# Four modulation blocks moved from the first feed-forward into the second mixer, and eight moved back in the third

## The reference

```python
def modulation(c, w, b):
    m = jnp.einsum("bd,de->be", jax.nn.silu(c), w) + b
    shift, scale, gate = jnp.split(m, 3, axis=-1)
...
for layer in range(DEPTH):                                   # first block: stages 0, 1 and 2, 3
    shift, scale, gate = modulation(c, ada_w[layer, 0], ada_b[layer, 0])
    h = x * (1.0 + scale) + shift
    y = hybrid_mixer(h, ...)                                 # in, SSD + MLA + gating, out
    x = layer_norm(DN_ALPHA * x + (1.0 + gate) * y, ...)
    shift, scale, gate = modulation(c, ada_w[layer, 1], ada_b[layer, 1])
    h = x * (1.0 + scale) + shift
    y = swiglu(h, ...) if layer % 2 == 0 else moe_swiglu(h, ...)
    x = layer_norm(DN_ALPHA * x + (1.0 + gate) * y, ...)
```

## Time and profile before

| | |
|---|---|
| median of 3 runs | 2105.08 us (2104.85 to 2108.06) |
| profiled execution, its own time | 2110.58 us |
| its span | 2108.7 us |
| mean granted clock of TensorE | 0.96 of full |
| busy share | TensorE 94%, VectorE 79%, ScalarE 56% |
| first feed-forward, first product to the next stage's input | 188.95 to 404.76 us |
| second mixer | 404.76 to 531.77 us |
| third mixer up to its last blocks of `wout2` | 1388.85 to 1530.55 us |

### The profile page before, as it was taken

The page is one execution under the profiler, slowest core; times in us unless marked ns, Lnnn a source line. Parts: engine busy times, 40 slices in busy tenths (PEclk is TensorE's granted clock), DMA queues, the critical chain, the costliest instruction groups (busy, mean ns, idle before and its releaser), DMA issues.

```text
span 2108.7 us, 28332 instructions
## 1 busy us (share of the span) xinstructions
PE 1979.9 (94%) x11530; PEld 1713.3 (81%) x11530; DVE 1673.0 (79%) x1753; ACT 1170.4 (56%) x1316; POOL 72.4 (3%) x121
## 2 busy tenths in 40 slices
PE   6989999999799999999999999878899999989999
PEld 6778899886678887887878888668689989869998
DVE  6777889887788998989898888878778886756444
ACT  3544334464567777777777777556444344654432
POOL 6001000000000000000000000000010000000000
PEclk9988999899899999999999999989789998989999
DMA  9754999644499999999999999824359994324552
GB/s 350 267 183 162 349 352 361 215 150 162 166 343 335 352 373 343 341 358 370 324 356 365 361 336 349 310 81 159 120 209 355 353 366 134 121 80 140 180 182 98
DMA packets 251210, 554.37 MB, mean 263 GB/s; under 512 B 10077, under 2 KB 75857, under 8 KB 251073
## 3 DMA queue, kind: packets, MB, share of 16 engines
q1 hardware_dynamic: 247252, 544.13, 72.3%
q0 software_dynamic: 3552, 8.29, 1.2%
q10 hardware_dynamic: 268, 0.07, 0.0%
HBM read 551.40 MB, written 1.05 MB: 262 GB/s over the span
## 4 chain that ended last, share of the span: by engine, by line
PE 75%; DVE 13%; ACT 6%; issue 3%; DMA 3%; SPq 0%; ACTq 0%; DVEq 0%
PE bank L499 22%; PE bank L501 21%; PE bank L500 21%; DVE ring_lo L1960 4%; ACT ring_hi L1263 3%; DVE acc L1900 2%; PE bank L888 1%; PE bank L581 1%; PE bank L550 1%; DMA ring<-in_ffn_w_dram 1%; PE bank L1088 1%; DVE work L2145 1%; DMA ring<-in_w_in_dram 1%; DMA ring<-in_ada_w_dram 1%; PE bank L527 1%
## 5 line engine op out<-in xcount | busy, mean ns | idle before, releaser
L1960 DVE TENSOR_TENSOR ring_lo<-ring,ring_hi 128x2048 fp32r<-128x2048 f32 x417 | 949.5, 2286 | 252.2 <-ACT ring_hi L1263 249.6
L1263 ACT ACTIVATE ring_hi<-ring 128x2048 fp32r<-128x2048 f32 x417 | 794.9, 1913 | 474.3 <-PE bank L501 232.1
L499 PE MATMUL bank<-hh,ring_hi 128*128 128x256 f32 x1152 | 330.3, 287 | 10.4 <-DVE ring_lo L1960 5.6
L500 PE MATMUL bank<-hl,ring_hi 128*128 128x256 f32 x1152 | 328.2, 285 | 0.0
L501 PE MATMUL bank<-hh,ring_lo 128*128 128x256 f32 x1152 | 328.2, 285 | 0.0
L501 PE MATMUL bank<-ring_hi,hl 128*128 128x256 f32 (+2 forms) x768 | 239.1, 311 | 0.0
L499 PEld LDWEIGHTS bank<-hh,ring_hi 128*128 128x128 f32 x1152 | 223.4, 194 | 13.6 <-DVE hl L2024 5.9
L499 PE MATMUL bank<-ring_hi,hh 128*128 128x256 f32 (+2 forms) x672 | 214.2, 319 | 15.6 <-DVE hl L2024 9.2
L499 PE MATMUL bank<-ring_hi,hgh 128*128 128x512 f32 (+1 forms) x576 | 220.4, 383 | 9.0 <-DVE ring_lo L1960 4.0
L500 PEld LDWEIGHTS bank<-hl,ring_hi 128*128 128x128 f32 x1152 | 223.5, 194 | 1.0 <-issue 0.5
L501 PEld LDWEIGHTS bank<-hh,ring_lo 128*128 128x128 f32 x1152 | 223.2, 194 | 0.0
(11 more groups left out here) (425 smaller groups left out, 2788.9 us busy)
## 6 DMA issues: line engine op xcount, KB each, us to landing
ring<-in_moe_w_dram SPq DMA_DIRECT2D x264, 1024.0 KB, 5.2
ring<-in_ada_w_dram SPq DMA_DIRECT2D x48, 1024.0 KB, 7.2
ring<-in_w_mod_dram SPq DMA_DIRECT2D x48, 1024.0 KB, 7.2
ring<-in_w_in_dram SPq DMA_DIRECT2D x40, 1024.0 KB, 6.1
ring<-in_ffn_w_dram SPq DMA_DIRECT2D x33, 1024.0 KB, 5.6
ring<-in_w_gate_dram SPq DMA_DIRECT2D x22, 1024.0 KB, 5.0
ring<-in_w_up_dram SPq DMA_DIRECT2D x22, 1024.0 KB, 5.1
ring<-in_w_down_dram SPq DMA_DIRECT2D x22, 1024.0 KB, 5.0
```

The source lines that it names most:

```text
L499: pe.matmul(ps, xh, wh, start=first, stop=False)
L500: pe.matmul(ps, xh, wl, start=False, stop=False)
L1263: act.activation(ring_hi[i % NH][:, 0:z], ring[n % NS][:, 0:z], ACT.Copy).then_inc(*s.hi(("hi", home(s, i), i)))
L1960: dve.tensor_tensor(ring_lo[n % NS][:, 0:z], ring[n % NS][:, 0:z], hi, ALU.subtract).then_inc(*s.lo(("lo", home(s, i), i)))
```

## The change

Three edits of order, none of arithmetic:

1. The four blocks of stage 3's shift (`mod 3 0 p`) leave the weave of the first feed-forward, which keeps 28 of 32. In the second mixer a new function `put_behind` places them with the four blocks of stage 3's gate (`mod 3 2 p`): behind its blocks 0, 2 and 4 one each, behind block 9 (`wout` 2) three, behind block 11 (`wout` 0) two. Three of them are taken out of the plan's order on VectorE by `one_modulation(3)`: one before `outputs()`, two behind it.
2. In the third mixer the eight blocks of stage 5's shift and scale stand two weight blocks later: one each behind blocks 10 to 14 and three behind the last. These three are multiplied by VectorE before the last two blocks of `wout2` are taken up.
3. `project(10)` in the third and fourth mixer makes the high half first.

```diff
--- before.py
+++ after.py
@@ -355,8 +355,16 @@
 
         WHOLE = [("wout", l, i) for l in range(2) for i in (2, 3)]
         put_blocks(weave(ffn_blocks((("ffn", 0), a["ffn_w1"][0], a["ffn_w3"][0], a["ffn_w2"][0])),
-                         mods((1, 2), (4, 0), (4, 1), (2, 0), (2, 1), (2, 2), (3, 0), (3, 1))))
-        put_blocks(weave(win_blocks(1) + rowblocks(("wout", 1), a["w_out"][1]), mods((3, 2))))
+                         mods((1, 2), (4, 0), (4, 1), (2, 0), (2, 1), (2, 2), (3, 1))))
+
+        def put_behind(blocks, behind, extra):
+
+            for i, b in enumerate(blocks):
+                n = behind[i] if i in behind else 0
+                put_blocks([b] + extra[:n])
+                extra = extra[n:]
+
+        put_behind(win_blocks(1) + rowblocks(("wout", 1), a["w_out"][1]), {0: 1, 2: 1, 4: 1, 9: 3, 11: 2}, mods((3, 2), (3, 0)))
         put_blocks(weave(ffn_blocks(*[(("moe", x), a["moe_w1"][0, x], a["moe_w3"][0, x], a["moe_w2"][0, x]) for x in range(8)]), mods((4, 2)), 6, 6))
         IN_MOE = [(4, 2)]
 
@@ -364,8 +372,7 @@
         for l in range(2):
             win2 = [(("win2", l, i), (kview(8, 256), krows(a["w_in_2"][l][:, 256 * i:256 * i + 256]))) for i in WIN2]
             blocks = win2 + rowblocks(("wout2", l), a["w_out_2"][l])
-            for i, b in enumerate(blocks):
-                put_blocks([b] + (mods((5, 0), (5, 1))[i - 8:i - 7] if l == 0 and i >= 8 else []))
+            put_behind(blocks, {10: 1, 11: 1, 12: 1, 13: 1, 14: 1, 15: 3}, mods((5 + 2 * l, 0), (5 + 2 * l, 1)) if l == 0 else [])
             put_blocks(weave(ffn_blocks((("ffn2", l), a["w_gate_2"][l], a["w_up_2"][l], a["w_down_2"][l])),
                              mods((5, 2), (6, 0), (6, 1), (6, 2), (7, 0), (7, 1), (7, 2)) if l == 0 else []))
 
@@ -1583,10 +1590,9 @@
             def mixer2(l, m):
                 M = ("m2", l)
 
-                def project(i, dst, *waits, at_once=False):
+                def project(i, dst, *waits):
                     summed(turn_of["win2", l, i])
-                    if not at_once:
-                        high_halves(main, ahead(turn_of["win2", l, i]))
+                    high_halves(main, ahead(turn_of["win2", l, i]))
                     act.wait_ge(*at(*M, "proj", i))
                     for z in waits:
                         act.wait_ge(*at(*z))
@@ -1651,10 +1657,9 @@
                 next(diff)
                 project(3, gb(1, 1))
                 squares(1)
-                project(10, vt(2), at_once=True)
+                project(10, vt(2))
                 values_in(2)
                 turn_group(0)
-                halves_for(10)
                 next(diff)
                 next(diff)
                 sd((*M, "qk", 1), stat(16, *M, "qk", 1))
@@ -1960,6 +1965,11 @@
                     dve.tensor_tensor(ring_lo[n % NS][:, 0:z], ring[n % NS][:, 0:z], hi, ALU.subtract).then_inc(*s.lo(("lo", home(s, i), i)))
                     done[0] += 1
 
+            def one_modulation(m):
+
+                if mods_left and mods_left[0][1] == m:
+                    gemv(mods_left.pop(0))
+
             def rstd(name, ss, n, eps):
                 settled()
                 dve.tensor_scalar(ss, ss, 1.0 / n, eps, ALU.mult, ALU.add).then_inc(*vec((*name, "var")))
@@ -2421,7 +2431,12 @@
                 spatial()
                 across_chunks()
                 late_features()
+                if l:
+                    one_modulation(3)
                 outputs()
+                if l:
+                    one_modulation(3)
+                    one_modulation(3)
                 mixed(M, range(2), "wout", l, None)
                 block("wout", 0)
                 block("wout", 1)
@@ -2548,6 +2563,8 @@
                 next(moba)
                 half_normed(1)
                 mixed(M, range(2), "wout2", l, evac)
+                for _ in range(3):
+                    one_modulation(5 + 2 * l)
                 block("wout2", 0)
                 block("wout2", 1)
```

## The result

| | before | with the change |
|---|---|---|
| median | 2107.83 us (8 runs, 2104.85 to 2109.97) | 2112.70 us (8 runs, 2111.10 to 2114.94) |
| ratio | 1 | 1.0022, 95% interval 1.0012 to 1.0033 |
| profiled execution, span | 2108.7 us | 2110.9 us |

The change makes the kernel 0.22% slower, 4.9 us; forecast were 6.2 us, or 2111.3 us. The kernel before, measured with more runs beside it, has a median 2.75 us above the one that I started from.

The account below looks back on a forecast made before the run. TensorE, busy 94% of the span, was taken as the floor; only its gaps and stage ends could move. Terms -6.4 + 6.5 + 6.1 = +6.2 us on 2105.08 gave 2111.3 us, range 2101.5 to 2116.5.

Parts of the forecast that it names:

- First feed-forward: Thinner weave: four TensorE gaps close (-4.6 us) and the stage end comes earlier (-1.8), -6.4 us in all.
- my bound of -8.5: First feed-forward's best case: also regains the 2 us TensorE lost at the lower clock after the last gap.
- Second mixer, start: Stage 3's first gate block stands before a VectorE low half, 2.57 us less a 1.02 wait: 1.5 us late.
- Second mixer, end: Two blocks before `wout` 1's low half: TensorE stalls 4.6 us, VectorE's residual comes 4.2 later; taken as +5.0 us.
- Third mixer: Lead from later modulation blocks is lost at the end, where the first `w_gate` load waits for `wout2` 0: +6.1 us.
- The lead of 3.9 us: Third mixer's head work runs 3.9 us earlier without two modulation blocks, read from the fourth mixer; bounds -2 and -5.1.
- Third edit: High half before `project(10)` is hidden in a ScalarE wait: 0 us, at most 1.9 us, twice, if not hidden.
- The rule on the price of a load: Skill gives 4.4 us for a lone 1 MB load; the forecast used the trace's 5.0 us instead.
- (a): Whole kernel about the same: terms nearly cancel at their good bounds, +0.9 us, 2106.0 us; chance 0.27.
- (b): Faster: first `w_gate` load doesn't bind, so the third mixer keeps its lead; -5.0 us, 2100.1 us; chance 0.13.
- (c): Slower by more: TensorE at low clock after each new wait, loads another 1 us late; +10.8 us, 2115.9 us; chance 0.11.
- (d): First feed-forward's thinner weave gives nothing, its gaps only move to other blocks; +12.6 us, 2117.7 us; chance 0.04.

Follow-up runs that it names:

- spread: Changed kernel with the second mixer's eight modulation blocks placed where VectorE waited, none between the low halves of `wout` 0 and 1; 2104.63 us, ratio 0.9982.
- first edit alone: Kernel before plus only the move of stage 3's shift blocks from the first feed-forward into the second mixer; 2108.41 us, ratio 0.9999.
- the kernel without the stall: Changed kernel with the second mixer's last two modulation blocks behind `wout` 1 in the plan, not before it; 2111.76 us, ratio 1.0019.
- third edit alone: Kernel before plus only the high half made before the evacuation of projection 10, third and fourth mixer; 2106.66 us, ratio 0.9997.
- The placement with 2 and 2: Changed kernel with two of the third mixer's modulation blocks behind `wout2` 3 and two, not three, behind the last block; 2106.71 us, ratio 0.9993.
- the spread and the third mixer as before: Changed kernel with second-mixer blocks where VectorE waited and the third mixer's blocks as in the kernel before; 2101.07 us, ratio 0.9963.
- both placements together: Changed kernel with second-mixer blocks where VectorE waited and third-mixer blocks 1, 1, 2, 1, 2, 1 behind blocks 10 to 15; 2105.81 us, ratio 0.9986.

## Why the prediction was right

**The stages, over all profiles.** Each stage, with the order of before and with that of the change, in the executions that had it (spread and other placements left out):

| stage | order of before | changed order | difference of means | forecast |
|---|---|---|---|---|
| first feed-forward | 217.0 to 217.6 (3) | 207.5 to 211.3 (10) | -8.1 | -6.4 |
| second mixer | 145.4 to 147.5 (3) | 153.6 to 155.4 (5) | +7.9 | +6.5 |
| third mixer | 162.3 to 165.9 (4) | 168.6 to 170.9 (5) | +5.5 | +6.1 |
| sum | | | +5.3 | +6.2 |

Each term has its sign and is within 1.7 us of its forecast, and the sum is near the measured 4.9. The errors are -1.7, +1.4 and -0.6, so that the sum is closer than its largest terms is luck; so is part of the nearness of 2111.3 to 2112.70, as the kernel before came out 2.75 us above the median that I had added to.

- **First feed-forward.** Right in kind: the small gaps closed. The single pair of profiles gives just the -6.4; over all of them it is -8.1, nearer to my bound of -8.5, in which TensorE doesn't fall to its lower clock behind the last gap. So it was in most of them: with the first edit alone the last gap is 1.83 us, not 2.78, and the products behind it (376.17, 376.40, 376.63) start 0.23 us apart, where they start 0.43 apart behind the 2.78. (The other bound, -4.5, was added up wrongly: -1.8 and half of 4.6 is -4.1.) What I had missed at the end is ScalarE's evacuation of `gate` (1.25 us at 372.57), which stands before the high half there.
- **Second mixer, start.** The 1.5 us were 1.4: the attention's first masked product that VectorE takes after its wait stands 50.4 us behind the start (449.44), 49.0 before (455.38).
- **Second mixer, end.** Landing of `wout` 1: forecast 514.3, on the clock of before with the start's shift 515.8; it is 509.33 + 7.33 = 516.7, 7.33 being the difference of the two starts. The residual: 516.65 + 7.33 = 523.98 against 521.3 + 1.5 = 522.8. The step that says what costs was right in kind. I gave two paths to the end, TensorE's stall (+3.3 to +5.2) and VectorE's residual (+4.2), and took a value between. Both are there and end within about half a microsecond of each other: the kernel without the stall gains nothing, as the residual stands where it was, and in the changed kernel itself the chain that ended last runs through the stall. (TensorE's end was 0.2 us off in its sum: 518.6 + 36 x 0.23 is 526.9.)
- **Third mixer.** The lead of 3.9 us was 3.9. The load: forecast 1536.5, which is 147.7 behind the start; it came at 145.9. With the third edit alone, order of before, `wout2` 0's last use shows at 150.0, 1.5 earlier than the 151.5 of the trace that I read it from, so most of that is not the change's. The landing took 5.1 (5.0 forecast), the residual stands 155.2 behind the start, forecast 156.9. That the term looks like 3.4 in the pair is the trace of before: in two of the three other executions of the same order the mixer takes 2.8 us less.
- **Third edit.** 0, as forecast.

**The rule on the price of a load.** The Trainium skill (DMA: Bandwidth & Descriptors, Anatomy of one DMA) would have a lone block at an estimated 4.4 us, by a fit that it gives for DMAs issued by GpSimd. These loads are SyncE's, and the new trace has 5.1 us, from the issue at 1533.43 to ScalarE's start at 1538.56, so the measured price stands.

**The rivals.** (a) and (b) fell to the `w_gate` load, which does bind. The placement with 2 and 2 issued it earlier than the order of before (137.3 us from the start, 141.5 before), which (b) took as enough, and the mixer took 164.4 us, where the order of before takes 163.9 on average. But the load then lands behind two others, 9.5 us after its issue instead of 5, and ScalarE starts on it 146.8 us behind the stage's start, against 146.6 in the trace of before, so it still binds. Whether the lead would be kept with the load out of the way no run here shows. (c), the lower clock after each new wait: the products behind the 5.86 us gap did run at it (0.63 us each and 0.43 apart from 514.28 to 517.69, 0.23 apart behind that), and the forecast held it to be part of the end. Stall and lower clock together cost the stage no more than the 0.4 us above, as VectorE's residual would have ended it then. (d): the thinner weave kept its gain.

## What to carry to other kernels

In a ring of slots a block's place in the list has two prices, its own load's and that of the block six places later: ask which block's last use releases the first load of the next stage, and count what stands between that load and the residual. A gap of TensorE at a stage's end is no price by itself if another engine's queue ends at the same time; taking it away alone gave nothing here, and shortening both paths gave 5 us. And take at least three profiles of a kernel before reading stage differences below 3 us, since executions of one kernel differ by that within a stage.

## What the runs showed of the hardware

**The same stage, two lengths.** The feed-forward behind the third mixer takes 203.7 to 205.2 us in ten executions and 209.2 to 209.6 in three of them, with the same instructions. Of two kernels whose orders agree there, the first edit alone and the third alone:

```profile
1546.11:1755.61 209.50, 203.13 (x1372) 188.40 (x1373) 170.44 (x138) 85.15 (x80) 1.44 (x2) 0.96 0.85 306
```

```profile
1547.68:1752.54 204.86, 200.78 (x1373) 187.64 (x1373) 170.40 (x138) 85.17 (x80) 1.44 (x2) 0.97 0.86 313
```

TensorE is busy 203.13 and 200.78 us at clocks of 0.96 and 0.97, and the loads move 306 and 313 GB/s. Whether slower loads or lost clock comes first stays open: no run here varies one alone.

**A normalization that takes longer beside a memset.** The last multiply-add of the norm before the feed-forward, for the first half of the tokens, takes VectorE 0.75 us, but 1.83 in the trace of before (1544.90, with a memset of GpSimd from 1545.22 to 1546.19) and 1.52 with the spread and the third mixer as before, with a memset over its start. That one, the memset beside it, and the usual one of the changed kernel:

```profile
1539.37 1.52 DVE L2020 TENSOR_SCALAR XN<-X,st 128x1024 f32<-128x1024 f32 x1
1539.36 0.97 POOL L2873 MEMSET QK<- 128x1024 f32 x1
1548.03 0.75 DVE L2020 TENSOR_SCALAR XN<-X,st 128x1024 f32<-128x1024 f32 x1
```

In the others a memset lay over it for 0.1 us or less, and it took 0.75, or for 0.3 us, and it took 0.85 (both placements together, 1538.12). The longer time goes with the overlap; no run moves the memset alone. It is one more microsecond by which stages differ from one execution to the next.
